# Gate products in the middle of a U tile, and the powers of two one tile earlier on ScalarE

## The reference, cut to what matters

```python
def peer_ffn(h, w_q, keys, u_tab, v_tab):
    ...
    gates = jax.nn.softmax(best_s, axis=-1).astype(h.dtype)
    ...
    def block(args):
        hb, eb, gb = args
        act = jnp.einsum('thkd,td->thk', u_tab[eb], hb)
        coef = gb * jax.nn.gelu(act, approximate=False)
        return jnp.einsum('thk,thkd->td', coef, v_tab[eb])
```

## Time and profile before

| what | value |
|---|---|
| median of three runs | 2869.01 us (2868.68 to 2871.35) |
| the profiled execution | 2868.51 us |
| its span, first to last instruction | 2866.8 us |
| TensorE busy, share of the span | 98% |
| VectorE, ScalarE, GpSimd busy | 87%, 48%, 33% |
| U tiles with gate products, first layer | from 580.07 to 926.01 us |
| the same, second layer | from 1972.75 to 2319.22 us |

### The profile page before, as it was taken

One profiled execution on the slowest core, in us unless ns is written; L12 is line 12 of the kernel. 1 busy time (PEld: TensorE's weight loads), 2 busy tenths in 40 slices (PEclk: granted clock), 3 DMA queues, 4 the chain that ended last, 5 costly groups with the idle time before them and its releaser, 6 DMA issues.

```text
span 2866.8 us, 49322 instructions
## 1 busy us (share of the span) xinstructions
PE 2810.2 (98%) x17864; PEld 2602.4 (91%) x17864; DVE 2495.0 (87%) x5020; ACT 1370.3 (48%) x2321; POOL 949.7 (33%) x773
## 2 busy tenths in 40 slices
PE   7999999999999999999999999999999999999998
PEld 4777789999999999999988788999999999999998
DVE  4667788999999799999987679999999979999998
ACT  3345124367777333334353532445777753333433
POOL 1000028733335244444400000684333434444342
PEclk9999999999999999999999999999999999999999
DMA  7434748989999899999932122698999999999996
GB/s 278 173 118 176 261 143 306 342 331 396 391 374 348 336 378 386 382 383 384 378 123 74 59 74 82 225 327 323 386 377 390 363 339 363 383 379 386 382 382 252
DMA packets 257143, 855.05 MB, mean 298 GB/s; under 512 B 26080, under 2 KB 59104, under 8 KB 250336
## 3 DMA queue, kind: packets, MB, share of 16 engines
q1 hardware_dynamic: 149280, 442.23, 41.9%
q0 software_dynamic: 98496, 381.73, 35.3%
q10 hardware_dynamic: 9216, 29.36, 2.5%
HBM read 777.06 MB, written 76.15 MB: 298 GB/s over the span
## 4 chain that ended last, share of the span: by engine, by line
PE 82%; DMA 6%; DVE 5%; ACT 3%; issue 2%; POOL 1%; SPq 0%; DVEq 0%; ACTq 0%; POOLq 0%
PE banks L1092 43%; PE banks L1627 27%; DMA w_raw<-wst 4%; PE banks L1588 3%; PE banks L1425 2%; DVE w_lo L1668 2%; ACT w_hi L806 1%; PE banks L1162 1%; PE banks L1108 1%; PE banks L1512 1%; DMA pj<-adaw 1%; DVE vacc L2180 1%; POOL w_lo L755 1%; PE banks L1266 0%; DMA activations<-act_out 0%
## 5 line engine op out<-in xcount | busy, mean ns | idle before, releaser
L806 ACT ACTIVATE w_hi<-w_raw 128x1024 fp32r<-128x1024 f32 x596 | 630.8, 1059 | 778.6 <-PE banks L1092 635.2
L1092 PE MATMUL banks<-hH,w_hi 128*128 128x352 f32 (+1 forms) x2528 | 873.4, 345 | 18.0 <-issue 9.0
L1668 DVE TENSOR_TENSOR w_lo<-w_raw,w_hi 128x1024 fp32r<-128x1024 f32 x522 | 638.4, 1223 | 254.2 <-ACT w_hi L806 238.2
L1092 PE MATMUL banks<-hH,w_lo 128*128 128x352 f32 (+1 forms) x2528 | 849.0, 336 | 0.0
L1092 PE MATMUL banks<-hL,w_hi 128*128 128x352 f32 (+1 forms) x2528 | 848.7, 336 | 0.0
L768 POOL DMA_INDIRECT ring<-v,gidx x320 | 393.6, 1230 | 627.1 <-DVE vacc L2180 536.5
L1092 PEld LDWEIGHTS banks<-hH,w_hi 128*128 128x128 f32 x2528 | 474.8, 188 | 68.3 <-issue 38.2
L1627 PE MATMUL banks<-c_lo_late,w_hi 128*128 128x352 f32 x1536 | 493.9, 322 | 0.0
L1092 PEld LDWEIGHTS banks<-hH,w_lo 128*128 128x128 f32 x2528 | 474.3, 188 | 19.5
L1092 PEld LDWEIGHTS banks<-hL,w_hi 128*128 128x128 f32 x2528 | 475.3, 188 | 17.3 <-issue 0.5
L768 POOL DMA_INDIRECT ring<-u,gidx x244 | 280.5, 1150 | 461.3 <-DVE gact L2168 441.8
(11 more groups left out here) (354 smaller groups left out, 3957.2 us busy)
## 6 DMA issues: line engine op xcount, KB each, us to landing
w_raw<-wst SPq DMA_DIRECT2D x596, 512.0 KB
activations<-act_out SPq DMA_DIRECT2D x124, 352.0 KB
act_in<-activations SPq DMA_DIRECT2D x62, 704.0 KB
gate_matrices<-stages ACTq DMA_DIRECT2D x64, 448.0 KB
gates<-gate_matrices SPq DMA_DIRECT2D x64, 448.0 KB
ada_buf<-adaw POOLq DMA_DIRECT2D x24, 1024.0 KB, 7.2
nrm<-adaw POOLq DMA_DIRECT2D x8, 1024.0 KB, 5.1
pj<-adaw POOLq DMA_DIRECT2D x7, 1024.0 KB, 7.3
```

The costliest lines, as they stand in the source:

```text
L806: nc.scalar.activation(w_hi[g % 2][:, :, :].rearrange("p a b -> p (a b)"), w_raw[:, g % RAWS, :], ACT.Copy).then_inc(s_wh, 1)
L1092: last = mm(bank[s][:, 0:t.stop - t.start], a[s][:, k, :], b[:, k, t], start=(k == 0 and a is w_hi and b is hH), stop=(k == KT - 1 and a i ...
L1668: v.tensor_tensor(w_lo[g % 2][:, :, :].rearrange("p a b -> p (a b)"), w_raw[:, g % RAWS, :], w_hi[g % 2][:, :, :].rearrange("p a b -> p (a ...
```

## The change

TensorE runs the gate products of tile n after the 12th of its 24 wide matmuls, and no longer after the last. ScalarE multiplies the powers into the one-hots for the quads of tile n+1 where it did so for those of tile n. VectorE's list is as it was. The two ways in which the loops over tiles 42 to 119 were written are now one function, `gates_of`; the loops' bounds and the waits' values are the same.

```diff
                 for n in range(N_KEYS):
-                    for q in quads_of(n):
+                    for q in quads_of(n + 1):
 
                         act.wait_ge(s_eq, l * QUADS + q + 1)
                         for t in range(QUAD):
...
-            def project(l, n, s, tokens=None):
+            def project(l, n, s, tokens=None, halfway=None):
...
                 for k in range(KT):
+                    if k == KT // 2 and halfway is not None:
+                        halfway()
                     for a, b in ((w_hi, hH), (w_hi, hL), (w_lo, hH)):
...
-                def u_tile(n, s):
-                    project(l, U0 + n, s, tokens=slice(TG, T))
+                def u_tile(n, s, halfway=None):
+                    project(l, U0 + n, s, tokens=slice(TG, T), halfway=halfway)
...
-                def gate_tiles(i, tiles):
-
-                    for j in range(tiles):
-                        u_tile(i * GATE_LOOP + (GATE0 + j), j % 2)
-                        for u in quads_of(GATE0 + j):
-                            pe.wait_ge(s_oh, l * QUADS + u + 1 + i * per)
-                            pe.wait_ge(s_bp, l * QUADS + u + 1 + i * per)
-                            pe.wait_ge(s_gv, l * QUADS + u + 1 + i * per)
-                            gate_quad(u)
...
+                def gates_of(n, i=0):
+
                     for u in quads_of(n):
-                        pe.wait_ge(s_oh, l * QUADS + u + 1)
-                        pe.wait_ge(s_bp, l * QUADS + u + 1)
-                        pe.wait_ge(s_gv, l * QUADS + u + 1)
+                        pe.wait_ge(s_oh, l * QUADS + u + 1 + i * per)
+                        pe.wait_ge(s_bp, l * QUADS + u + 1 + i * per)
+                        pe.wait_ge(s_gv, l * QUADS + u + 1 + i * per)
                         gate_quad(u)
+
+                with pe.Fori(0, GATE_LOOPS) as i:
+                    for j in range(GATE_LOOP):
+                        u_tile(i * GATE_LOOP + (GATE0 + j), j % 2, lambda: gates_of(GATE0 + j, i))
+                for n in range(GATE0 + GATE_LOOPS * GATE_LOOP, GATE1):
+                    u_tile(n, n % 2, lambda: gates_of(n))
```

## The result

The changed kernel is slower: 2891.9 us (median of four runs, 2890.64 to 2894.09), against 2870.18 (2868.68 to 2873.0) for the kernel before on the same chip. The ratio is 1.0077 with an interval of 1.0065 to 1.009. The profiled executions agree: the span grew from 2866.8 us to 2888.9, by 22.1 us, where the prediction had 27.

What follows compares the result with a forecast made beforehand. TensorE, busy 98% of the span, was taken as the bound. Per layer 11.9 + 1.3 + 0.6 = 13.8 us; twice that less 0.5 is 27, so 2869 + 27 = 2896 us, range 2884 to 2918.

Steps and rivals of the forecast that it cites:

- The limit: TensorE's idle time in the two stretches: removing waits can win back at most 2.6 us, 0.09% of the time.
- The boundary: First wide matmul after a quad holds TensorE 0.25 us, not 0.16, at tile's end or middle alike: no cost.
- Powers ahead of w_hi: On ScalarE, eight powers before double tiles delay w_hi and the eviction freeing TensorE's PSUM bank: 11.9 us per layer.
- The first product: In the middle of tile 42, TensorE waits for scaled one-hots until 579.89; cost 1.3 us per layer.
- The one-hots' deadline: VectorE's scaled one-hots, due 1.97 us earlier, cause five waits in crowded two-gather tiles: 0.6 us per layer.
- VectorE as the bound: Rival: any added tenth in a VectorE hand-over is paid by TensorE; 2920 us, or 2912; chance 0.14.
- The sum: Whole kernel: 13.8 us per layer, twice that less 0.5 is 27 us, giving 2896 us, 0.9% slower.
- Only the opening and the next tile's bank: Rival: powers done in time, only tile 42's wait and the product after a double tile cost; 2878 us, chance 0.10.
- Nothing: Rival: the gate evictions are early enough, so the time stays 2869 us within 0.2%; chance 0.06.
- faster by the rhythm: Rival: moving the quad turns TensorE's 70 long tiles short, gaining 12 us; 2857 us, chance 0.04.

Runs made afterwards that it cites:

- mid_only: Changed kernel with the products still in mid-tile but the powers back in their old place on ScalarE; 3132.16 us, ratio 1.0911.
- after_6th: Changed kernel with the products after the 6th wide matmul of a tile, not the 12th; 2961.78 us, ratio 1.0319.
- powers_only: Kernel before with only the powers for tile n+1 moved early on ScalarE, products still at the tile's end; 2884.66 us, ratio 1.0044.
- three_banks: Changed kernel with three PSUM banks in turn for the quads' products in place of two; 2884.23 us, ratio 1.0047.

## Why the prediction was right, step by step

*The limit.* The prediction had 2.6 us as all that waits could give back, so that only the costs mattered. It held in what it was used for: no kernel came out below before. As a figure it was low, for two reasons. Busy time hides part of each wait (by starts there were 4.1 us in the two stretches), and it left out the tiles behind them, of which more below.

*The boundary* costs nothing: the first wide matmul behind a quad now holds TensorE for 0.25 us in mid-tile (724.29 to 724.54), as it did at the tile's start.

*Powers ahead of w_hi*, 11.9 us per layer, was the step that carried the sum, and it was right in place and near in size: 13.3 and 12.6 us were measured. Second quads wait 9.48 and 9.04 us over the ten double tiles of a layer where 8.9 were predicted: 0.78 to 0.87 us in six, 0.95 to 1.17 in the other four, at tiles 49, 57, 113 and 117 (0.8 in seven and 1.1 in three). The next tile's product waits 0.30 to 0.40 (0.3), 728.58 at tile 74 in place of 728.18. w_hi starts 1.2 to 1.3 us after the tile's end ahead of those six doubles, 1.4 to 1.6 ahead of those four, and elsewhere mostly 0.26, at most 0.54 (predicted 1.2, and 0.25 to 0.35). The Trainium skill (TensorE: Matmul & The Clock Gate, Architectural detail) has ScalarE's queue strictly first in, first out; the chain at tile 73 agrees, as w_hi starts when the eighth power is done, 1.22 us after the end of the tile that it otherwise follows by 0.26.

*The first product.* Predicted at 579.89 after 1.7 us of wait; the timelines of VectorE and TensorE have

```profile
579.42 0.69 DVE L2195 TENSOR_TENSOR oneh<-oneh,gate_parts 128x1024 f16<-128x1024 f16 x1
```

```profile
580.16 0.62 PE L1590 MATMUL banks<-oneh 128*128 128x128 bf16 x8 [1.51 <-DVE oneh L2195]
```

The wait is 1.67 us in each layer by the starts. Tile 43 starts at 582.58, 1.2 us later than before if the 0.3 us by which the changed kernel was late already is taken off (1.3 predicted).

*The one-hots' deadline*, 0.6 us per layer in five waits: eight single-quad tiles wait for their one-hots in the first layer, 1.6 us in all, and six in the second, 0.9, each 0.07 to 0.36 us and all in the crowded places. So this was of the right kind and small, if larger than walked. The slack of the old order that the prediction gives here, 2.1 us, was 2.6: the quad of tile n, 0.46 us, stood behind that tile's end too. No term hangs on it. VectorE as the bound is refuted at the middle of the tile: of the waits, 1.9 and 1.5 us are for its one-hots, 1.5 of them the opening's. At the 6th matmul that rival comes true.

*The sum.* By starts of w_hi (ScalarE's timeline of the kernel before, after tile 40 and after tile 119)

```profile
572.73 1.06 ACT L806 ACTIVATE w_hi<-w_raw 128x1024 fp32r<-128x1024 f32 x1 [2.01 <-PE banks L1092]
...
926.27 1.06 ACT L806 ACTIVATE w_hi<-w_raw 128x1024 fp32r<-128x1024 f32 x1 [1.00 <-PE banks L1092]
```

and the same of the changed one

```profile
573.04 1.06 ACT L806 ACTIVATE w_hi<-w_raw 128x1024 fp32r<-128x1024 f32 x1 [2.01 <-PE banks L1094]
...
940.46 1.06 ACT L806 ACTIVATE w_hi<-w_raw 128x1024 fp32r<-128x1024 f32 x1 [2.53 <-PE banks L1094]
```

the first layer's stage grew by 367.42 - 353.54 = 13.9 us, and the second's by 13.4. Less tile 119's quad, that is 13.2 and 12.8 (seen one tile further on), for 13.8 predicted. The added waits, 14.7 and 13.2 us, are the prediction's terms and a little more. Old waits went with the change too, 2.9 us in the two stretches, where the prediction counted 0.5. Beside the waits stands a shorter rhythm in the first stretch (616 spacings of 164 ns or more between wide matmuls where there were 748, some 8 ns each, 1.1 us); in the second it is as it was (792 and 791).

*Where 5 us of the forecast's 27 went.* The stages made 26.0 of the 27. Of these, 3.8 us come back behind the stage, in the seven tiles after tile 120, 2.0 in the first layer and 1.8 in the second, which leaves 22.2; the span grew by 22.1. The sum took for granted that a delay at the stage's end stays to the end of the kernel; that is the step that was off in size. In the kernel before these tiles have waits of their own. Its chain, behind the first stretch:

```profile
935.94 1.24 DVE w_lo L1668
...
937.24 11.64 DMA w_raw<-wst
...
948.90 1.07 ACT w_hi L806
...
950.07 1.24 DVE w_lo L1668
...
951.39 7.84 PE banks L1092 x48
```

and the same place in the chain of the changed kernel:

```profile
938.94 31.83 PE banks L1094 x201
970.77 14.31 PE banks L1622 x89
```

Before, a weight transfer of 11.64 us ends late and TensorE waits about 0.9 us for it; the other 1 us is the long rhythm, in some 140 of 190 spacings of the first layer's tail. In the second layer it is mostly three waits, 1.4 us in all. After, there is no wait here and the spacing is the short one throughout, in both layers.

Whether that follows from the change was not tested, but the kernels sort by it. From w_hi after tile 120 to w_hi after tile 127, the changed kernel, mid_only and after_6th, whose stages grew by 13 us or more, have no wait in either layer; all others, whose stages grew by 8.5 or less, and the kernel before wait 0.4 to 2.5 us in both. So the waits may go because the stage before them is slower and its supplies get ahead; that is argued and not shown. The rhythm doesn't sort so: after_6th has the long one throughout. What sets it stays open.

*The rivals.* "Only the opening and the next tile's bank" fell with the second quads' waits. "Nothing" and "faster by the rhythm" fell with the sum; the rhythm did move in one of the two stretches, by about a tenth of what that rival needed. (The chances given for what lies below the range, 0.10, 0.06 and 0.04, add up to 0.20, not to 0.17.)

*What the prediction did not see* is that the late w_hi is a cost of its own. It charged the eight powers once, through the bank. powers_only and three_banks show a second path, through w_lo and the next one-hots, which the bank's wait covers. In powers_only it costs 6.1 and 5.3 us per layer. In three_banks 8.0 and 7.2 are left, seen one tile further on, and less the opening's 1.2 and what single tiles waited for one-hots in the changed kernel that is again some 5 us. It changed no number of this forecast, but it would have made the forecast for either repair too low, as my expectation for powers_only was.

## What to carry to other kernels

When a step is moved forward in an in-order queue, ask what is behind it, not only whether its own data is early enough: the powers were needed sooner, and four of them ahead of w_hi cost almost nothing, but eight held back w_hi, which starts the next round for two other engines. A stage whose tiles vary is priced tile by tile: a tile with one quad had room, and the ten double ones made most of the cost. Before repairing the wait that ends last, work out when the next one would end; here it was so close behind that removing the first won only 5.5 to 6 of 13 us.

## What the runs showed of the hardware

Equal matmuls ran in one of two spacings, and a quad between them could switch it. TensorE's timeline in the changed kernel, ahead of tile 73's quads and behind them:

```profile
719.64 0.33 PE L1094 MATMUL banks<-hH,w_hi 128*128 128x352 f32 x1
719.80 0.33 PE L1094 MATMUL banks<-hL,w_hi 128*128 128x352 f32 x1
...
724.54 0.32 PE L1094 MATMUL banks<-hL,w_hi 128*128 128x352 f32 x1
724.69 0.32 PE L1094 MATMUL banks<-hH,w_lo 128*128 128x352 f32 x1
```

From 719.64 to 722.47 seventeen spacings take 2.83 us, 0.167 each; from 724.54 to 728.02 twenty-two take 3.48, 0.158 each, at the same granted clock of 1.00. Nothing that I ran chose between the two. Short waits hardly lowered the clock here: in mid_only, with 1.34 us of waiting in each 5.81 us, the mean granted clock from 600 to 1050 us was 0.98.
